# Attention by pairs of heads over all query blocks, the sink column written once per pair, value matmuls of 128 columns, context blocks between latent ones

## What is computed

```
# latent queries, blocks of 128: keys of the window (+/-128 tokens) and all 256 context keys, one sink logit a head
p = softmax(concat([s_loc, s_ctx, s_sink], axis=-1))
o = p[..., :SPAN] @ vb + p[..., SPAN:SPAN + L] @ v_ctx
# context queries (layer 0 only): context keys and the sink
p = softmax(concat([s, s_sink], axis=-1))[..., :L];  o = p @ v_c
```

## Time and profile before

| | |
|---|---|
| median of 3 runs | 1543.95 us (1543.67 to 1544.62) |
| the profiled execution | 1543.87 us, its span 1542.1 us |
| TensorE busy | 1503.8 us, 98% of the span |
| VectorE / ScalarE busy | 900.1 us (58%) / 520.9 us (34%) |
| attention, layer 0 (first `turn` to the statistics after the last values) | 216.9 to 299.1 us |
| attention, layer 1 | 1056.1 to 1117.1 us |

### The profile page before, as it was taken

How to read it: one execution, slowest core, us unless ns; L and a number is a source line. 1 busy time by engine, 2 the same in 40 slices (tenths; PEclk the granted TensorE clock), 3 DMA queues, 4 the chain that set the end, 5 groups by cost and what they waited for, 6 DMA issues and landing times.

```text
span 1542.1 us, 22646 instructions
## 1 busy us (share of the span) xinstructions
PE 1503.8 (98%) x8910; PEld 1230.0 (80%) x8910; DVE 900.1 (58%) x1375; ACT 520.9 (34%) x789; POOL 103.5 (7%) x149
## 2 busy tenths in 40 slices
PE   5999999999999999999999999999999999999997
PEld 3876775688888888888888889777679888888886
DVE  3684679667666425665853466768787533333335
ACT  3311458624222112222112244148844322221232
POOL 0043200040000000000000000520030000000000
PEclk9999999999999999999999999999999999999999
DMA  9683510013333123333432123520023333333322
GB/s 358 224 228 80 207 53 28 2 55 110 123 111 121 57 94 133 126 122 137 150 109 68 44 69 106 149 61 15 29 69 96 96 96 96 95 95 96 96 92 85
DMA packets 39864, 161.14 MB, mean 104 GB/s; under 512 B 5617, under 2 KB 6001, under 8 KB 33649
## 3 DMA queue, kind: packets, MB, share of 16 engines
q1 hardware_dynamic: 35856, 148.72, 28.7%
q0 software_dynamic: 3936, 11.45, 2.8%
HBM read 149.76 MB, written 2.10 MB: 98 GB/s over the span
## 4 chain that ended last, share of the span: by engine, by line
PE 90%; DVE 5%; DMA 2%; issue 1%; ACT 1%; SPq 1%; DVEq 0%; ACTq 0%
PE banks L536 76%; PE banks L565 3%; PE banks L692 3%; PE banks L680 2%; PE banks L707 2%; DMA ada_raw<-in_w_ada 2%; PE banks L472 1%; PE banks L742 1%; PE banks L522 1%; PE banks L504 1%; DVE neg_max L1254 1%; DVE ada_sum_context L1221 0%; DVE x L1230 0%; PE banks L481 0%; DMA raw<-in_w_gu 0%
## 5 line engine op out<-in xcount | busy, mean ns | idle before, releaser
L536 PE MATMUL banks<-h_both,w_high 128*128 128x512 f32 (+1 forms) x2496 | 507.3, 325 | 3.2 <-DVE tmp L1182 1.1
L823 ACT ACTIVATE w_high<-raw 128x1024 fp32r<-128x1024 f32 (+2 forms) x182 | 186.2, 1023 | 709.4 <-PE banks L536 696.1
L536 PEld LDWEIGHTS banks<-h_both,w_high 128*128 128x128 f32 x2496 | 374.8, 189 | 54.6 <-issue 17.0
L1136 DVE TENSOR_TENSOR w_low<-raw,w_high 128x1024 fp32r<-128x1024 f32 (+2 forms) x182 | 217.3, 1194 | 228.6 <-ACT w_high L823 225.1
L536 PE MATMUL banks<-h_both,w_low 128*128 128x512 f32 (+1 forms) x1248 | 301.8, 323 | 0.0
L536 PEld LDWEIGHTS banks<-h_both,w_low 128*128 128x128 f32 x1248 | 192.1, 189 | 18.3
L1181 DVE COPY shift_product<-banks 128x2 f32<-128x2 f32 x78 | 12.3, 158 | 193.5 <-PE banks L536 183.0
L536 PE MATMUL banks<-h_normal_low,w_high 128*128 128x512 f32 x304 | 118.3, 389 | 0.0
L536 PE MATMUL banks<-h_normal_high,w_high 128*128 128x512 f32 x304 | 118.3, 389 | 0.0
L536 PE MATMUL banks<-h_normal_high,w_low 128*128 128x512 f32 x304 | 118.3, 389 | 0.0
L536 PE MATMUL banks<-ff_high,w_high 128*128 128x512 f32 x352 | 90.2, 337 | 0.0
(11 more groups left out here) (198 smaller groups left out, 2030.1 us busy)
## 6 DMA issues: line engine op xcount, KB each, us to landing
raw<-in_w_gu SPq DMA_DIRECT2D x88, 512.0 KB, 3.5
ada_raw<-in_w_ada SPq DMA_DIRECT2D x21, 1024.0 KB, 5.6
raw<-in_w_dn SPq DMA_DIRECT2D x32, 512.0 KB, 3.5
raw<-in_w_mix SPq DMA_DIRECT2D x28, 512.0 KB, 4.7
ada_in_ff<-in_w_ada SPq DMA_DIRECT2D x12, 1024.0 KB, 5.5
raw<-in_w_out SPq DMA_DIRECT2D x16, 512.0 KB, 3.5
ada_first<-in_w_ada SPq DMA_DIRECT2D x7, 1024.0 KB, 14.7
raw<-in_w_dn SPq DMA_DIRECT2D x16, 384.0 KB, 3.0
```

The source lines that it names most:

```text
L536: last = mm(bank[:, 2 * slot + bk, to:to + b - a], weights[w][:, k0_w + k, :], rhs[:, k0_rhs + k, a:b], start=(k == 0 and n == 0), stop=(k ...
L823: last = f(wH[j][:, at, :], raw[j][:, at, :], ACT.Copy)
L1136: last = tt(wL[j][:, at, :], raw[j][:, at, :], f32(wH[j][:, at, :]), ALU.subtract)
```

## The change

- A group is now a **pair of heads** on one block. The order is pair by pair (4 pairs), over all blocks, in layer 0 in the order 0, 1, 4, 2, 3, 5: 24 groups of 2 units, and 16 in layer 1. The units and their keys are the same, the order is new.
- A value matmul streams one head (128 columns) per column half where it streamed two (256): twice as many matmuls, each half as wide. `probT` becomes a ring of 4 groups of 2 heads where it was 2 of 4.
- The scores end at a fixed column of the slot, so that the sink column lies at the same place for every unit of a head; it is written only in the first block of each pair (8 units of each layer) and read by all. For that the scores of blocks 0 and 3 cross a bank, and their 512-column key matmuls become two of 256.
- `group_out` copies 128 columns twice as often, and the steps of the extras are tables by layer: layer 1 keeps its steps, layer 0 spreads them from step 1 to step 44 (before, to step 25).

```diff
-KEY_TILES = [[(0, 1, 4, 5)], [(0, 2, 4), (1, 5)], [(1, 3, 5), (2, 4)], [(2, 3, 4, 5)], [(4, 5)], [(4, 5)]]
+KEY_TILES = [[(0, 1), (4, 5)], [(0, 2, 4), (1, 5)], [(1, 3, 5), (2, 4)], [(2, 3), (4, 5)], [(4, 5)], [(4, 5)]]
+BLOCK_ORDER = [[0, 1, 4, 2, 3, 5], [0, 1, 2, 3]]
+PT_RING = 4
@@ queries
-    return [(g, b, [t for tiles in KEY_TILES[b] for t in tiles]) for g in range(KV)
-            for b in range(TB if layer == 0 else NB)]
+    return [(pair, b, [t for tiles in KEY_TILES[b] for t in tiles]) for pair in range(HEADS // 2)
+            for b in BLOCK_ORDER[layer]]
@@ score_place
-            at = 1024 * (u % 2) + (P if len(keys) == 5 else 0)
+            at = 1024 * (u % 2) + 6 * P - P * len(keys)
@@ steps of the extras, (layer 0, layer 1)
+        ROPE_AT, Q_HIGH_AT, Q_LOW_AT = ((1, 3, 6, 8), (1, 3, 5, 7)), (9, 8), ((12, 14), (9, 10))
+        HIGH_AT, LOW_AT = ((12, 14, 18, 20), (9, 10, 11, 12)), ((15, 18, 20, 24), (12, 13, 14, 16))
+        SQUARE_AT, ADD_AT = ((24, 25, 30, 32), (13, 14, 16, 17)), ((27, 31, 33), (15, 18, 19))
+        CONV_HIGH_AT, CONV_LOW_AT = ((33, 36, 38, 42), (18, 19, 20, 21)), ((37, 39, 43, 44), (22, 23, 24, 25))
@@ TensorE, scores
-                    if i == 0 and q == len(qs) // 2:
-                        pe.wait_ge(q_ok, CT * (layer + 1))
+                    if i == 0 and b == BLOCK_ORDER[layer][0]:
+                        pe.wait_ge(q_ok, CT * layer + pair + 1)
...
-                    parts.append((first + P * len(keys), 1, onesb[:], sink_rows[:, layer, h:h + 1]))
+                    if b == BLOCK_ORDER[layer][0]:
+                        parts.append((first + P * len(keys), 1, onesb[:], sink_rows[:, layer, h:h + 1]))
@@ TensorE, values
                     if m == 0:
-                        pe.wait_ge(pt_ok, GRP * (n + 1))
+                        pe.wait_ge(pt_ok, 2 * (n + 1))
...
                         if n >= 2:
                             pe.wait_ge(a_ok, n - 1)
                     for odd in range(2):
-                        last = mm(bank[HD * odd:HD * odd + HD, BC + n % 2, 0:2 * P], V[:, keys[m], HD * g:HD * g + HD],
-                                  PT[:, n % 2, m, 2 * odd:2 * odd + 2, :].rearrange("p h q -> p (h q)"),
+                        last = mm(bank[HD * odd:HD * odd + HD, BC + n % 2, 0:P], V[:, keys[m], d0:d0 + HD],
+                                  PT[:, n % PT_RING, m, odd, :],
@@ TensorE, the loop
-                    if n >= GRP:
-                        q = n // GRP - 1
+                    if n >= 2:
+                        q = n // 2 - 1
                         for m in range(len(qs[q][2])):
-                            if m * GRP // len(qs[q][2]) == n % GRP:
+                            if m * 2 // len(qs[q][2]) == n % 2:
                                 values(q, m)
@@ VectorE, group_out
-                    nc.vector.tensor_copy(aT[:, 2 * g:2 * g + 2, P * b:P * b + P],
-                                          bank[:, BC + n % 2, 0:2 * P].rearrange("p (h q) -> p h q", h=2)).then_inc(a_ok, 1)
+                    nc.vector.tensor_copy(aT[:, pair, P * b:P * b + P], bank[:, BC + n % 2, 0:P]).then_inc(a_ok, 1)
```

More of the change, by code:

```diff
@@ L647, in attention @@
                 qs = queries(layer)
-                order = [(q, i) for q in range(len(qs)) for i in range(GRP)]
-                unit0 = GRP * group_index[layer, 0]
+                order = [(q, i) for q in range(len(qs)) for i in range(2)]
+                unit0 = 2 * group_index[layer, 0]
                 def scores(n):
                     q, i = order[n]
-                    g, b, keys = qs[q]
+                    pair, b, keys = qs[q]
                     u = unit0 + n
@@ L661, in scores @@
                         pe.wait_ge(slot_free[n], USES[layer, "ob"])
-                    if i == 0 and q == len(qs) // 2:
-                        pe.wait_ge(q_ok, CT * (layer + 1))
+                    if i == 0 and b == BLOCK_ORDER[layer][0]:
+                        pe.wait_ge(q_ok, CT * layer + pair + 1)
                     if u >= 2:
                         pe.wait_ge(exp_ok, u - 1)
-                    first = 1024 * (u % 2) + (P if len(keys) == 5 else 0)
+                    h = 2 * pair + i
+                    first = 1024 * (u % 2) + 6 * P - P * len(keys)
                     parts, at = [], first
                     for tiles in KEY_TILES[b]:
-                        parts += [(at, P * len(tiles), Q2[:, g * GRP + i, P * b:P * b + P],
-                                   key_columns(K2[:, g, part, :], tiles)) for part in range(2)]
+                        parts += [(at, P * len(tiles), Q2[:, h, P * b:P * b + P],
+                                   key_columns(K2[:, h // GRP, part, :], tiles)) for part in range(2)]
                         at += P * len(tiles)
@@ L696, in values @@
                 def values(q, m):
-                    g, b, keys = qs[q]
+                    pair, b, keys = qs[q]
                     n = group_index[layer, q]
+                    d0 = HD * (2 * pair // GRP)
                     if m == 0:
-                        pe.wait_ge(pt_ok, GRP * (n + 1))
+                        pe.wait_ge(pt_ok, 2 * (n + 1))
                         if q == 0:
@@ L880, in conv_norm @@
             def conv_norm(layer, n, width):
[L883 to L885 removed]
+                if n in HIGH_AT[layer]:
+                    part = HIGH_AT[layer].index(n)
+                    split_high(layer, "qkv", 2, part // 2, part % 2)
+                if n == Q_HIGH_AT[layer]:
                     q_high(layer, LAST_Q, width)
[L887 to L888 removed]
+                if n in SQUARE_AT[layer]:
+                    k = SQUARE_AT[layer].index(n)
                     act.wait_ge(ln_s, CT * layer + k + 1)
                     square("cn", layer, k, cv[:, k, 0:width])
[L891 to L892 removed]
+                if n in CONV_HIGH_AT[layer]:
+                    k = CONV_HIGH_AT[layer].index(n)
                     f(conv_high[:, k, 0:width], cv[:, k, 0:width], ACT.Copy, scale=col("g_conv", k, layer)).then_inc(conv_hi, 1)
@@ L1283, in attention @@
                         divide(n + 2)
-                    if n in (12, 13, 14, 16):
-                        part = (12, 13, 14, 16).index(n)
+                    if n in LOW_AT[layer]:
+                        part = LOW_AT[layer].index(n)
                         split_low(layer, "qkv", 2, part // 2, part % 2)
-                    if n == 15:
+                    if n == ADD_AT[layer][0]:
                         m = sq_index[layer, "cn"]
@@ L1304, in attention @@
                             in1=f32(conv_high[:, k, 0:width]), op0=ALU.mult, op1=ALU.subtract).then_inc(conv_lo, 1)
-                    if n % GRP == 0 and n >= 2 * GRP:
-                        group_out(n // GRP - 2)
+                    if n % 2 == 0 and n >= 4:
+                        group_out(n // 2 - 2)
                 group_out(len(qs) - 2)
```

32 lines of the change are left out of this document (14 added, 18 removed).

## The result

The changed kernel takes 1547.68 us (median of 10 runs, 1546.73 to 1548.75) where the kernel before took 1544.15 in the same comparison (10 runs, 1543.36 to 1546.34). The ratio is 1.0019, with a 95% interval of 1.0011 to 1.0027: 2.9 us slower, between 1.7 and 4.2. The profiled execution has a span of 1545.6 us, where it was 1542.1.

The account below looks back on a forecast made before the run. TensorE's stream, busy 98% of the span, was taken as the bound, with ScalarE's copy loop limiting attention steps. Layer 0 +3.7 - 1.4, layer 1 -0.2 gave +2.1 us on 1543.95: 1546.0 us, range 1541.0 to 1550.5.

Parts of the forecast that it names:

- copy loop: Attention steps: next transpositions wait until ScalarE copies the previous unit from PTB; 1.63, 1.46, 1.04 us for 5, 4, 2 keys.
- the term for the stalls: Layer 0 attention: extras on ScalarE stall steps by 4.6 us where it was 6.0, so -1.4 us.
- The sink: Scores, both layers: 64 fewer sink matmuls save 0.01 us each, 0.6 us, since they run inside a gap that stays.
- Rival 3: Scores: each removed sink matmul gives back its spacing, 0.10 us more for 48 of them, 1541.2 us; chance 0.15.
- Narrow value matmuls: Values: 128-column passes keep the pace, 0.108 us for 0.216; visits cost 0.37, 0.58 or 0.80 us for 1 to 3 tiles.
- Rival 2: Values: weight loads set the pace of 128-column passes, 136 ns for 108, +7.6 us, 1553.6 us; chance 0.08.
- The order: Layer 0's new step sequence: 20.3 us a pair, 79.9 us in all, 3.7 more than before, 3.0 of it idle.
- step sum: Layer 0 attention: the steps' predicted lengths added up without stalls, 79.9 us after the change, 76.2 before.
- A step is the longer of its work and this loop: Attention stages: each step takes TensorE's own work or the copy loop, whichever is longer; no other limit priced.
- The price of one extra: Layer 0, ScalarE: an extra of 0.88 us exceeds the mean slack of 0.55 by 0.35, at 13 places, 4.6 us.
- Rival 1: Layer 0: stalls grow to 9.0 us, as copy-bound steps leave ScalarE least room, 1550.5 us; chance 0.23.
- The new steps of the extras: Layer 0: extras moved to new steps leave 4.6 us of stalls where there were 6.0, -1.4 us.

Follow-up runs that it names:

- experiment 2: The changed kernel with the sink column written again in every unit: 1548.09 us, ratio 1.0021 to the kernel before.
- experiment 4: The changed kernel with layer 0's blocks in order 0 to 5, the sink in every unit and the extras at their old steps: 1544.23 us, 0.9997 of before.
- experiment 8: The changed kernel with layer 0's four weight splits and four squares on ScalarE cut to 8 columns, computation left out: 1546.20 us, 1.0008 of before.
- experiment 1: The changed kernel with layer 0's blocks in natural order 0 to 5, nothing else undone: 1542.86 us, 0.9987 of before.
- experiment 3: The changed kernel with layer 0's extras back at their old steps, block order kept: 1546.53 us, 1.0012 of before.
- experiment 10: The changed kernel with layer 0's blocks in the order 0, 4, 1, 5, 2, 3: 1546.33 us, 1.0013 of before.

## Why the prediction came out as it did

1546.0 us was predicted, +2.1; it came to 1547.68, +3.5 by the medians and 2.9 (1.7 to 4.2) by the ratio. The copy loop held, and the term for the stalls was too small.

- **The place.** All of it in layer 0: +3.2 us in that stage, where +2.3 was predicted, and +0.2 in layer 1, where -0.2 was. From first `turn` to the statistics, by the start of each, layer 1 has 61.07 before and 61.14 after, so that its difference is 0.1 us.
- **The sink** was taken at 0.01 us each and is worth nothing that can be seen (experiment 2: 85.4 us either way). Rival 3, 0.10 us each, is out. The estimate of 1.6 us for all 64 from the Trainium skill ("TensorEngine Tiling (Array Packing)", Instruction Overhead) would be 1.0 us for the 40 in layer 0, 0.6 of it in steps that the copy loop doesn't hold, and no run shows it. The same page of the Trainium skill has the drain when the tiling mode changes (Key Properties), and the trace agrees: 0.21 us from mask to values, of which the 256 columns of the mask are 0.11.
- **Narrow value matmuls** keep their pace: 0.59 and 0.80 us for two and three tiles, 0.58 and 0.80 predicted, and experiment 4 is shorter than before. Rival 2 is out. The group copy takes 0.28 us, as taken, and isn't among the larger waits.
- **The copy loop** is as predicted in block 0 (1.47 for 1.46) and 0.05 to 0.06 longer in block 2 (1.69 for 1.63, 1.68 in experiment 8).
- **The order** was to cost some 4 us by the prediction's own steps (in the natural order, blocks 0 to 5, they give 3.32, 3.66, 3.38, 3.10, 3.00 and 2.88, 19.3 us a pair where the change has 20.3) and costs 5.3 (experiment 1), 4.6 with light extras. The way from the kernel before, in layer 0: pairs and narrow matmuls -0.8 (experiment 4), new steps in the natural order -1.3, the order +5.3, together +3.2.
- **The stalls, the mis-sized term.** The prediction had 4.6 us over the step sum of 79.9 and put all of them down to extras; measured are 85.4 - 79.9 = 5.5. Read from the timelines, ScalarE's extras are 3.4 of them (experiment 3), of which experiment 8 confirms 1.2 by a run. The other 2.1 us aren't theirs. The step that failed is "A step is the longer of its work and this loop". There is a third limit: the scores of step n wait for the exponential of unit n + 2, and that one stands on ScalarE behind the copy of the step before. Where a step turns 2 keys its scores come so early that they meet it: block 4's first step takes 1.89 to 1.95 us for 1.72 in all four pairs, 0.9 us together, and block 5's first at least 1.84 for 1.65 in the three pairs where it issues scores, 0.6 us. The remaining 0.6 is in pieces of 0.05 or so, most of them in the copy loop. So the extras were put too dear by 1.2 us and the third limit at nothing, and the two errors cancelled in part: that the sum came within 0.9 us of the 5.5 is luck.
- **The price of one extra** was a mean, 0.35 us at 13 places. The traces have 0.1 to 0.6 us at the six places in front of the second step of blocks 0 and 2, 1.1 at one, 0.1 at one, and nothing at five. The prediction had the cause in hand, "0.19 us (block 0, first)" of slack, and averaged it away. Rival 1 had this right, that copy-bound steps leave ScalarE least room, but not that nearly all of each extra shows; its point, 5.7 us of stalls, was nearly reached.
- **The new steps of the extras** were held to relieve ScalarE (-1.4 us of stalls). Experiments 3 and 4 show that this holds only in the natural order; in the change's own order the old steps are 1.3 us better. The timelines put that down to the six places. The tables also move VectorE's extras, no run moved ScalarE's alone, and a table without these six places wasn't tried.

The change without its order (experiment 1) is a little faster than both kernels, 0.9987 (0.9978 to 0.9996) of before; with a second place for the transpositions it is 0.9988, the same.

## What to carry to other kernels

Where two engines hand units back and forth, list for each step every resource that its first instruction waits for, and what stands ahead of the releasing instruction on its own engine: here the copy and the exponential are one queue, and opening the wait for the one moved it to the other. Before you shuffle long and short units, look which step issues the work of which unit at the run-ahead distance: with a distance of four units and groups of two, the long transpositions met the shortest scores and the shortest values. A sum of steps finds that, but not the waits between engines: it was 7.4 us off for the order of experiment 10. Price extra work step by step and not by a mean: the same kind of extra cost nothing in one step and up to 0.6 us in another. And try each part of a change alone: here one line of it cost 5.3 us and hid 2.1 us of gain in the rest.

## What the runs showed of the hardware

- 38 one-column matmuls placed between a full-array matmul and a load for column strips took no time that the windows can tell (85.4 us with and without): the gap from the 256-column mask to the values is 0.22 us with the sink in it and 0.21 without. For a context unit, which has no mask, scores to values are 0.46 us with the sink and 0.43 without (260.50 to 260.93 in the kernel after).
- A value matmul of 128 columns has a load of 137 ns in the rows, and yet a pass of both column halves, with two such loads, takes 0.11 us: a key tile is two such passes, and three tiles take 0.80 us where two take 0.59. Four loads of 137 ns have a row of 0.20 us in the timeline, so they overlap each other. The group of these loads, min, median and max ns:

```profile
L712 PEld LDWEIGHTS banks<-probT,v_tokens x640: 132/137/137, 221.1 to 1120.4; 128*64 128x64 f32 x160
```

- The scores that wait for an exponential start only behind the read of its sum: at 267.96, 0.05 us behind the end of that row (267.71 + 0.20) and 0.14 behind the end of the exponential's own (267.03 + 0.79). The first two such waits of the stage have 0.05 us too.
